# The first transfers on one queue in another order, and the first five chunks of a two-layer model interleaved in place of four

## What is computed

```
ada = c_act @ w_ada + b_ada
shift, scale, gate = jnp.split(ada, 3, axis=-1)
u = x * (1.0 + scale[:, None, :]) + shift[:, None, :]
proj = jnp.einsum("bsd,dp->bsp", u, w_in)
...
q = jnp.einsum("bsr,rk->bsk", rms_norm(q_lat, q_norm_g), w_uq)
kv = jnp.einsum("bsr,rk->bsk", rms_norm(kv_lat, kv_norm_g), w_ukv)
k_pe = apply_rope(k_rope, cos, sin)[:, :, None, :]
```

## Time and profile before

| | us |
|---|---|
| median of three runs | 2256.07 |
| lowest, highest | 2256.03, 2262.36 |
| the profiled execution | 2257.16 |
| its span, first to last instruction | 2255.0 |
| TensorE busy | 2188.2 |
| VectorE busy | 1437.1 |
| GpSimd busy | 1084.1 |
| ScalarE busy | 865.0 |

### The profile page before, as it was taken

The page is one execution under the profiler, slowest core; times in us unless marked ns, Lnnn a source line. Parts: engine busy times, 40 slices in busy tenths (PEclk is TensorE's granted clock), DMA queues, the critical chain, the costliest instruction groups (busy, mean ns, idle before and its releaser), DMA issues.

```text
span 2255.0 us, 31166 instructions
## 1 busy us (share of the span) xinstructions
PE 2188.2 (97%) x11306; PEld 1802.2 (80%) x11306; DVE 1437.1 (64%) x2299; ACT 865.0 (38%) x1458; POOL 1084.1 (48%) x1273
## 2 busy tenths in 40 slices
PE   8999999999999999999988999999999999999998
PEld 6788877888688887788777888887787887888886
DVE  3598858764558885887678766638576776433322
ACT  3534353222553335222354433434344344333321
POOL 3565436665356544676525544432434344343443
PEclk9999999999999999999999999999999999999999
DMA  8322227663332222666313222232424333222222
GB/s 275 94 87 82 75 76 247 234 213 118 103 94 85 75 75 89 227 204 201 111 55 103 103 80 99 96 111 102 133 74 152 96 111 99 59 73 75 70 80 75
DMA packets 97576, 259.87 MB, mean 115 GB/s; under 512 B 10400, under 2 KB 20000, under 8 KB 97312
## 3 DMA queue, kind: packets, MB, share of 16 engines
q1 hardware_dynamic: 76224, 212.51, 29.4%
q10 hardware_dynamic: 21216, 45.51, 5.6%
HBM read 237.01 MB, written 20.97 MB: 114 GB/s over the span
## 4 chain that ended last, share of the span: by engine, by line
PE 54%; issue 21%; POOL 14%; DVE 7%; ACT 2%; DMA 1%; ACTq 0%; POOLq 0%; DVEq 0%
PE bank L2199 17%; PE bank L2200 17%; PE bank L2201 16%; POOL t L479 13%; DVE t L1855 3%; DVE t L1316 1%; PE bank L2436 1%; DVE t L1320 1%; PE bank L2445 1%; PE bank L2612 1%; DMA t<-w_ada 1%; PE bank L2285 0%; DVE t L1810 0%; DVE t L1852 0%; PE bank L2456 0%
## 5 line engine op out<-in xcount | busy, mean ns | idle before, releaser
L479 POOL TENSOR_TENSOR t<-t,t 128x256 fp32r<-128x256 f32 x1172 | 1005.2, 889 | 1038.8 <-ACT t L553 1038.3
L2199 PE MATMUL bank<-t,t 128*128 128x512 f32 (+1 forms) x3056 | 1170.7, 383 | 25.7 <-DVE t L1316 5.8
L2200 PE MATMUL bank<-t,t 128*128 128x512 f32 (+1 forms) x3056 | 1142.4, 374 | 0.0
L2201 PE MATMUL bank<-t,t 128*128 128x512 f32 (+1 forms) x3056 | 1141.8, 374 | 0.0
L2199 PEld LDWEIGHTS bank<-t,t 128*128 128x128 f32 x3056 | 576.0, 188 | 154.6 <-issue 11.1
L2201 PEld LDWEIGHTS bank<-t,t 128*128 128x128 f32 x3056 | 575.1, 188 | 105.3
L2200 PEld LDWEIGHTS bank<-t,t 128*128 128x128 f32 x3056 | 576.1, 189 | 103.3 <-issue 4.3
L553 ACT ACTIVATE t<-t 128x1024 fp32r<-128x1024 f32 x302 | 317.0, 1054 | 275.9 <-PE bank L2201 245.5
L1651 DVE SCALAR_TENSOR_TENSOR t<-t,t,t 128x512 f32<-128x512 f32 x240 | 217.2, 905 | 7.5 <-ACT t L735 1.0
L1382 DVE SCALAR_TENSOR_TENSOR t<-t,t,t 128x512 f32<-128x512 f32 x168 | 158.9, 965 | 43.3 <-ACT t L840 29.9
L1320 DVE SCALAR_TENSOR_TENSOR t<-t,bank 128x512 f32<-128x512 f32 x112 | 76.7, 685 | 135.8 <-ACT t L1273 59.8
(11 more groups left out here) (256 smaller groups left out, 1684.0 us busy)
## 6 DMA issues: line engine op xcount, KB each, us to landing
t<-blocks SPq DMA_DIRECT2D x306, 512.0 KB, 3.6
t<-w_ada SPq DMA_DIRECT2D x160, 256.0 KB, 4.2
t<-w_ada SPq DMA_DIRECT2D x14, 512.0 KB, 10.3
xm_park<-t ACTq DMA_DIRECT2D x16, 384.0 KB, 2.3
s_park<-t ACTq DMA_DIRECT2D x16, 384.0 KB, 2.5
t<-xm_park ACTq DMA_DIRECT2D x16, 384.0 KB, 4.8
t<-s_park ACTq DMA_DIRECT2D x16, 384.0 KB, 5.3
xc_park<-t ACTq DMA_DIRECT2D x16, 256.0 KB, 2.2
```

Source lines behind the costliest of these rows:

```text
L479: low = pool.tensor_tensor(w_lo[slot][:, part], w_raw[slot][:, part], w_hi[slot][:, part].bitcast(F32), ALU.subtract)
L2199: pe.matmul(out, wh, xh, start=start, stop=False)
L2200: pe.matmul(out, wh, xl, start=False, stop=False)
L2201: return pe.matmul(out, wl, xh, start=False, stop=stop)
```

## The change

SyncE issues block 0, then shift and scale half 0 of group 0, then block 1, then shift and scale half 1, x(0), x(1), block 2, block 3. The scale halves of group 0 leave ScalarE's queue. Groups 1 to 3 follow as before, with block 4 now behind x(3) and block 5 behind x(7). `first_four` becomes `first_five`: chunk 4 joins the other four, the list of pairs is written anew, and at the end the three query chunks are finished ahead of the two key and value chunks. On ScalarE the splits move: block 2 ahead of uH(1), blocks 3 and 4 ahead of uH(2), block 5 ahead of uH(4). The copy of kv_lat 0 out of its bank goes behind the three squares of q_lat.

```diff
--- before.py
+++ after.py
@@ -405,23 +405,21 @@
 
             sp.dma_start(c_in[:], io["c_cols"]).then_inc(c_landed, 16)
             for g in range(4):
-                if g == 0:
-                    first_shift(g, 0)
-                    first_shift(g, 1)
-                    first_block(0)
-                else:
-                    for half in range(2):
-                        first_shift(g, half)
-                        first_scale(g, half)
+                for half in range(2):
+                    if g == 0:
+                        first_block(half)
+                    first_shift(g, half)
+                    first_scale(g, half)
                 first_x(2 * g)
                 first_x(2 * g + 1)
                 if g == 0:
-                    first_block(1)
-                if g < 2:
-                    first_block(2 + g)
-            for b in range(RING + 1, 2 * RING):
-                sp.wait_ge(weights_lo, b - RING + 1)
-                first_block(b)
+                    first_block(2)
+                    first_block(3)
+                if g in (1, 3):
+
+                    b = RING + (g + 1) // 2
+                    sp.wait_ge(weights_lo, b - RING + 1)
+                    first_block(b)
             sp.dma_start(tmp[2][:].bitcast(I32), io["positions"].partition_broadcast(128)).then_inc(pos_landed, 16)
             sp.dma_start(vec[:, FIRST_VEC:], io["vectors"][:, FIRST_VEC:]).then_inc(vec_landed, 16)
             sp.dma_start(mask[:], io["causal"]).then_inc(causal_landed, 16)
@@ -554,11 +552,6 @@
                     split[0] += 1
 
 
-            def first_scale(half):
-
-                tiles = io["w_ada"][16 + 4 * half:16 + 4 * half + 4].rearrange("t p c -> p t c")
-                act.dma_start(ada_first[0][SCALE][half][:], tiles[:, :, 0:W_ADA]).then_inc(scale_landed[0][half], 16)
-
             def first_u(j):
 
                 if j % 2 == 0:
@@ -569,14 +562,12 @@
 
             act.dma_start(vec[:, 0:FIRST_VEC], io["vectors"][:, 0:FIRST_VEC]).then_inc(first_vec_landed, 16)
             act.dma_start(ident[:], io["ident"]).then_inc(ident_landed, 16)
-            first_scale(0)
-            first_scale(1)
             act.wait_ge(c_landed, 16)
             act.activation(c_t[:], c_in[:], ACT.Tanh, scale=0.5).then_inc(act_done, a("c_tanh"))
             split_to(2)
             for j in range(KT):
-                if j in (2, 4):
-                    split_to(RING + j // 2 - 1)
+                if j in (1, 2, 4):
+                    split_to((3, 5, 6)[j // 2])
                 first_u(j)
             split_to(2 * RING)
 
@@ -659,13 +650,10 @@
                         for i in range(KT):
                             layer_out(l - 1, i)
                         split_to(B_QL(l) + j + 1 + RING)
-                if l == 0:
-                    evac(kv_lat[:, 0, :], banks[3][:], (l, "kv_lat", 0), None)
                 for j in range(3):
                     square(tmp[U_TMP[j]][:], q_lat[:, j, :], "q_lat", j, None)
-                if l:
-                    evac(kv_lat[:, 0, :], banks[3][:], (l, "kv_lat", 0), B_KVL(l))
-                else:
+                evac(kv_lat[:, 0, :], banks[3][:], (l, "kv_lat", 0), B_KVL(l) if l else None)
+                if l == 0:
                     act.wait_ge(dve_done, Dn("rope_angle"))
                     act.activation(rope[64:128, :], tmp[4][64:128, :], ACT.Sin).then_inc(act_done, a("rope_sin"))
                     root_ahead()
@@ -2239,7 +2227,7 @@
                             mm.then_inc(pe_done, p(*labels[n]))
                             cp.also("block", b + n)
 
-            def first_four(banks, labels):
+            def first_five(banks, labels):
 
 
                 def step(k, n):
@@ -2260,19 +2248,19 @@
                 stay_busy(2)
                 first_columns(0)
                 stay_busy(8)
-                steps((0, 0), (0, 1), (1, 0), (1, 1))
+                steps((0, 0), (0, 1), (1, 0), (1, 1), (0, 2), (1, 2))
                 first_rows_of(1)
-                steps((0, 2))
+                steps((0, 3))
                 first_columns(1)
-                steps((1, 2), (2, 0), (2, 1), (2, 2), (3, 0), (3, 1), (3, 2))
+                steps((1, 3), *((k, n) for k in (2, 3) for n in range(4)))
                 first_rows_of(2)
-                steps((0, 3))
+                steps((0, 4))
                 first_columns(2)
-                steps((1, 3), (2, 3), (3, 3), *((4, n) for n in range(4)), (5, 0))
+                steps((1, 4), (2, 4), (3, 4), *((4, n) for n in range(5)), (5, 0))
                 first_rows_of(3)
                 steps((5, 1))
                 first_columns(3)
-                steps((5, 2), (5, 3), *((k, n) for k in (6, 7) for n in range(4)))
+                steps((5, 2), (5, 3), (5, 4), *((k, n) for k in (6, 7) for n in range(3)), *((k, n) for n in (3, 4) for k in (6, 7)))
 
             def fold_quarters(l):
 
@@ -2374,8 +2362,7 @@
                     u_chunk(banks[4], B_QL(l) + 2, (l, "q_lat", 2))
                     u_chunk(banks[3], B_KVL(l), (l, "kv_lat", 0))
                 else:
-                    first_four([banks[0], banks[1], banks[4], banks[3]], [*((l, "q_lat", j) for j in range(3)), (l, "kv_lat", 0)])
-                    u_chunk(banks[6], B_KVL(l) + 1, (l, "kv_lat", 1))
+                    first_five([banks[n] for n in (0, 1, 4, 3, 6)], [*((l, "q_lat", j) for j in range(3)), *((l, "kv_lat", j) for j in range(2))])
                 for j in range(3):
                     pe.wait_ge(act_done, A(l, "q_lat_sq", j))
                     sum_quarters(banks[2], tmp[U_TMP[j]], j == 0, j == 2, (l, "q_sq", j))
```

## The result

| | before | changed |
|---|---|---|
| median us (6 runs each) | 2257.56 | 2269.11 |
| lowest, highest | 2256.03, 2262.36 | 2266.71, 2270.76 |
| span of the profiled execution | 2255.0 | 2266.5 |
| TensorE busy | 2188.2 | 2194.3 |

The account below looks back on a forecast made before the run. TensorE, busy 97% of the span, was taken as the bound, so new waits count in full: 6.6 + 2.7 + 2.7 = 12.0 us on 2256.1 gave 2268.0 us, range 2262.5 to 2272.5.

Parts of the forecast that it names:

- Part 1: Scale halves leave ScalarE's queue: first real product at 16.6 to 18.7 instead of 21.68, 3.0 to 5.1 us won only here.
- Part 2: Five chunks in place of four: same products regrouped, short TensorE waits before 24 us, costed at nothing.
- Part 3, the landing: Block 5, split ahead of uH(4) but loaded last behind x(7), lands at 42.5 us as before.
- The wait of 6.6 us: TensorE, through at 38.6, waits for uL(4) until 45.2 because uH(4) stands behind block 5's split.
- Harmless: Splitting block 4 ahead of uH(2): uL(2) serves at 28.2, against 29.53 before, so no cost.
- The first fall of the clock: Half clock behind the new wait for uL(4), ahead of group 3's rows, delaying the chain by 2.7 us.
- The angles, 8.8 us: Rope angles on VectorE behind uL(7), no longer covered by the fifth chunk, taken at 8.8 us as before.
- From the angles' end to the reciprocal's, 4.4 us: Sine, table load, split of block 6, root and reciprocal ahead of the spread, taken at 4.4 us.
- The second wait: TensorE waits 3.8 us, 65.0 to 68.8, at the query norm's spread, with a 2.7 us clock fall behind.
- the small stall: Rival: block 5 lands 2.8 us sooner, with one fall: 6.5 us lost, 2262.6 us; chance 0.08.
- the missing stall: Rival: the wait for block 5 does not bind and the earlier start counts: 2253.0 us; chance 0.05.
- The one-fall case: Rival: the clock falls only behind the first new wait, 6.6 + 2.7 = 9.3 us, 2265.4 us; chance 0.25.

Follow-up runs that it names:

- e3: Kernel before with only group 0's loads reordered on SyncE's queue; four chunks together, splits and blocks 3 to 5 unchanged: 2254.80 us, ratio 0.9989.
- e1: Changed kernel with ScalarE's split of block 5 moved back behind uH(7), loads untouched: 2261.49 us, ratio 1.0018.
- e2: Changed kernel with block 5 loaded right behind block 4, ScalarE's order kept: 2262.28 us, ratio 1.0021.
- e8: The kernel of e5 measured again on another occasion: 2260.16 us, ratio 1.0011.
- e5: e2 with the root taken right behind the sums of squares on ScalarE and VectorE's sign multiplication moved later: 2261.13 us, ratio 1.0014.
- e7: Changed kernel with block 5 loaded still later, behind positions, vectors and causal mask: 2269.45 us, ratio 1.0058.
- e4: Changed kernel with filler products in three TensorE waits, ahead of u(2), u(4) and the spread: 2265.06 us, ratio 1.0030.
- e6: e5 with 9 filler products in TensorE's wait ahead of the products for u(2): 2258.19 us, ratio 1.0003.
- e9: e3 with filler products between the halves of the first group's rows and ahead of u(2): 2254.86 us, ratio 0.9983.

## Why the prediction was right, and where its steps were off

The direction and the mechanism held: ScalarE waits for block 5 ahead of uH(4), and the time rises by what that wait and the falls of the clock cost. The total fell close to the forecast partly by luck. Its terms for the start come to 9.5 us where 12.0 was forecast, with two of them mis-sized in opposite directions, and 2 us that no term names were added behind the start. Against its steps:

- **Part 1.** The second half of group 0 landed near 13.0 (12.8 forecast), the first product came at 18.23 (16.6 to 18.7). "Only here" was right for the changed kernel; e3 shows that 2.6 us of it are kept where nothing behind takes them.
- **Part 2** held. TensorE waited 0.41 us at 22.03 for block 2's low part, and the rows of group 1 started at 23.59 without a wait.
- **Part 3, the landing.** The split of block 5 started at 42.64, forecast 42.5 for the landing. This term carried the sum and was right to 0.1 us. An estimate from the Trainium skill's 358 GB/s ("DMA: Bandwidth & Descriptors", Specifications) had put it at 40.8. The rate was not at fault, as a window of the changed kernel shows:

```profile
2.50:42.60 40.10, 33.33 (x303) 26.97 (x303) 8.83 (x21) 8.69 (x11) 15.22 (x20) 0.91 1.07 361
```

The last figure, 361 GB/s, gives 14.5 MB in these 40.1 us, 0.8 more than the 13.7 MB up to block 5. Most of these 0.8 MB must be of the transfers issued behind block 5, from 35.60 on, while it was on its way. e1 and e2 show the mechanism from two sides.
- **The wait of 6.6 us.** It was 3.79 us. TensorE came to u(4) at 42, not 38.6: the split of block 4 began at 26.52 (25.5 forecast for the landing), the wait for u(2) was 2.42 us, and the clock fell behind it, for a wait shorter than I had priced one. None of this moved the end, since block 5 set it. "Harmless" was the right word for the changed kernel and the wrong one for e2 and e8, in whose profiles this fall is paid.
- **From uH(4) to TensorE** 2.2 us (43.61 to 45.79) and not 1.67: uL(4) took 1.23 us beside GpSimd's work on block 5, where 0.69 stood.
- **The first fall of the clock.** From the resumption to the rows of group 3 it took 6.65 us where 4.2 was counted at full clock: 2.45 lost, 2.7 forecast.
- **The angles, 8.8 us, was the first mis-sized term**: 5.5 (58.65 to 64.19). The steps are shorter because GpSimd is idle beside them; the last section has the rows.
- **From the angles' end to the reciprocal's, 4.4 us, was the second**: 5.9 (64.19 to 70.06). I took the rope angles for what the spread waits on, with ScalarE ready behind them. In the kernel before that held: ScalarE had loaded the sine's table while the angles still ran (to 57.44).

```profile
55.30 1.28 ACT L670 ACT_TABLE_LOAD   x1
```

In the changed kernel ScalarE had the copies and squares of q_lat and the copy of kv_lat 0 to do behind the query chunks, and was free only at 64.42. The same load starts at 64.43, behind the angles' end, and its 1.28 us with the 0.2 ahead of it are the 1.5 us that this term lacked. The binding chain went over ScalarE, and e2 against e1 shows it: 1.8 us less of angles, 0.3 less at the spread. e5 shows that another order on ScalarE removes that wait.
- **The second wait** was 1.91 us, 3.8 forecast, and the clock fell behind it all the same; it cost 1.6 (9.5 at the table load less 7.9 at the spread), 2.7 forecast.
- **The sum** up to there is 9.5, forecast 12.0: 0.6 more for the later resumption, 0.25 less for the first fall, 3.3 less for the angles, 1.5 more behind them, 1.1 less for the second fall. The other 2 us of the 11.6 arise behind 100 us, in code that is the same. In the ten profiles the difference to before grows by 0 to 6 us between the first table load and the last. In two of these profiles it goes with the clock: between the table loads near 326 and 568 us the difference grows by 2.0 in e2's and shrinks by 2.0 in e7's, and the granted clock from 350 to 400 reads 0.93 in e2, 1.00 in e7 and 0.97 in before. It is a matter of the execution and not only of the kernel: e5 and e8, one kernel, grow by 4.5 and 1.7. Nearly all lean one way, and the one profile of before that they are held against is itself 0.9 us below the median of the first set, so some of it is that profile's good fortune. The medians of the changed kernel, e2, e4 and e7 lie 1.3 to 2.4 us above what the start's share gives, that of e5 3.6; e1 and e6 lie 0.1 and 0.7 above, e3, e8 and e9 0.6 below. Why the median of the changed kernel has 2 us more is open, and so the closeness of 2268.0 to 2269.11 is partly luck.

Of the rivals, the small stall and the missing stall fell with the landing at 42.6. The one-fall case, 9.3 us, was the nearest in size to what the start shows, but not in its cause: both falls came.

Parts of the loss by the runs: the wait for block 5 with the fall behind it some 7 us (7.6 in e1, 6.8 in e2). The wait at the spread was taken away by e5 (0.8 us, 2.4 when run again as e8), and the fall at u(2) by e6 (2.9 us of median, of which the profiles account for 1.6). The order of the loads by itself is a gain of 3.2 (e3).

## What to carry to other kernels

When work is moved ahead on an engine that runs in program order, look up the landing of everything that it waits for, and not only its duration: one microsecond of splitting cost some seven because its block was the last in the queue. "Order of need" has to be checked on every consumer's own instruction order, not on the products alone. And when a piece of cover is merged into what it covered, list each engine's work between the last product and the next wait; the bound may be on another engine than the one with the longest row.

## What the runs showed of the hardware

**VectorE slows beside GpSimd.** The same step of the angles (line 1406 before, 1394 now), 64 x 512 in float32, took 0.85 us before, with GpSimd busy for 5.77 of the 6 us from 48 to 54, and 0.49 in the changed kernel, with GpSimd at 0.00 from 58 to 64; the cast 0.85 and 0.42; the step with two tensor inputs 1.13 (3.40 for three) and 0.71 (2.14 for three). The neighbour decides it and not the kernel. In e1 GpSimd works from 52.09 to 55.71, and the steps take 0.85 up to there and 0.49 behind; in e2 it is idle, and the same first steps take 0.49. Saturated transfers do not do it: uL took 0.69 us at 28.78 in the kernel before, with 358 GB/s and GpSimd idle, and 1.23 at 28.39 in the changed one, with 346 GB/s and GpSimd busy. The windows of before and of after, columns as in the earlier trace rows:

```profile
48.00:54.00 6.00, 6.00 (x28) 4.97 (x27) 5.79 (x7) 3.78 (x7) 5.77 (x7) 1.00 0.20 43
```

```profile
58.00:64.00 6.00, 6.00 (x28) 4.98 (x27) 5.66 (x11) 3.43 (x7) 0.00 (x0) 1.00 0.00 1
```

The Trainium skill ("GPSIMD Engine Reference", 1. Specifications) says that the two share their interfaces to SBUF and contend where VectorE works in a two-port mode or reads two tensors from SBUF; these runs agree, and give the size, a factor of 1.6 to 2.0. Whether the steps that read one tensor run in such a mode, no run shows. A duration read from a trace holds only beside the same neighbour.

**The clock falls on short waits.** I had one case, 3.57 us. In the changed kernel's profile the granted clock fell to half behind waits of 2.06, 2.42 and 1.91 us as well; 2.44 us in e5's profile did not bring it down, 2.76 in e8's did. The length of the wait alone does not settle it: 2.63 us in e4's profile left the clock up, and the same wait of 1.91 us at the spread was followed by a fall in the changed kernel and in e2 and by none in e7. Filling such waits with useless products went with 4.0 us less in e4 and 2.9 in e6, and with nothing in e9, where a transfer set the pace.
